# A pooling's means and differences on GpSimd, and eight modulation tiles used between its sums

## The chip, the cores and the metric

The kernel runs on one core of a Trainium2 chip. A core has TensorE (PE, matmuls), VectorE (DVE), ScalarE (ACT), GpSimd (POOL) and SyncE (SP), which run at the same time and wait for each other through semaphores. The metric is the time of one execution in microseconds (us). Data lie feature-major: 128 partitions by time steps, here T = 256.

## The reference, cut to what matters

Two network blocks follow each other on a 256 x 1024 input. The change lies in the second layer of the first block, a multi-scale pooling mixer, and in the modulation of the second block:

```python
z = h @ p["w_in"]                       # "ou" (u) and "og" (g): 16 tiles of 128 features each
u, g = jnp.split(z, [W_POOL], axis=-1)
# for each group of 512 features with its window w in (2, 4, 8, 16), in each row of 64 steps:
lo = jnp.clip(t - w // 2, 0, n); hi = jnp.clip(t + w // 2, 0, n)
d = (s[hi] - s[lo]) / cnt - u           # s is the running sum: window mean minus the value
y = einsum(d, p["w_grp"]) * p["scale"]  # "grp"
out = (y * jax.nn.silu(g)) @ p["w_out"] # "oa", "ob"
```

Second block: `mod = silu(c) @ w_mod + b_mod` and, for its first two parts, the same matrix again with `silu(c_ctx)`.

## The kernel before

**Weight tiles.** All weight matrices come as one stream of tiles of 128 x 1024 numbers (512 KB), in the order of the list ORDER, through a ring of six buffers `raw`. SyncE's queue loads tile n once tile n - 6 is finished on TensorE (semaphore tile_done). ScalarE rounds each tile to w_hi (L904, helper `highs`), VectorE takes w_lo = raw - w_hi (L1277, helper `lows`), and TensorE does each product in three parts, 24 matmuls for one tile (L547 to L549, helper `thirds`). A tile's product stands in one of four PSUM banks until ScalarE has emptied it (semaphore ps_free; `emptied` waits for that). On VectorE, `ahead(name, t)` makes all w_lo up to the tile four places behind (name, t).

**ou and og.** TensorE does ou 0 to 3 side by side, then ou 4 to 15 and og 0 to 15 one after the other, then the statistics of the context (two matmuls on sqx, which wait for GpSimd's sum), then grp 0 to 7 (L684), which needs the differences d_in (semaphore d_ready), and then oa and ob. ScalarE empties ou tile t into opad (L1117), a buffer with 8 zero columns on each side of each row of 64, and og tile t through SiLU into og (L1127).

**Pooling.** VectorE works in four groups of four ou tiles (L1656 to L1667). For group g it waits until tiles 4g to 4g + 3 are emptied, with the w_lo's of tiles 4g + 4 to 4g + 7 made on the way, and then `window(g)` adds opad to itself, shifted, in 1, 2, 3 or 4 steps (L1291 writing win0 and win1 in turn). A multiplication by 1/count gives the mean (L1291 writing d_in), and a subtraction of opad gives the difference (L1667).

**Modulation.** GpSimd's queue loads 80 modulation tiles (512 KB each, L436) into four slots modw, each load once the slot's last tile is used (modw_used). VectorE uses a tile by multiplying it with a row of silu(c) and summing along the free dimension. Tiles 32 to 47 (groups 8 to 11, here "modulation tiles 0 to 15") are used twice (L1648): into `dump` with the context's row and into modw with the other row. VectorE does so once in each of og 0 to 15, behind the w_lo of tile t + 4; for og 12 to 15 that w_lo doesn't exist, since the tiles four places behind are grp's. Behind this VectorE makes vr (L1610), multiplies grp's products with og (L1685) and takes y_lo (L1696).

**GpSimd's sums.** GpSimd also adds up squares for statistics (`add_up`, L458). Those of the second context (sqx) stand in its queue behind the loads of group 10. ScalarE makes these squares ahead of og 10 (L1125), when all four differences are done, since sqx lies over win0 and win1.

Of the kernel before, what the change touches and what calls it, by code (L numbers as in the profile page):

```python
# [22 lines left out]
ALU = mybir.AluOpType  # L23
ACT = mybir.ActivationFunctionType

P = 128
D = 1024
T = 256
KT = D // P
# [80 lines left out]
MOD_ORDER = list(range(MOD_TILES // MOD_SLOTS))  # L110
MOD_AT = {g: n for n, g in enumerate(MOD_ORDER)}


PARAMS = [
    ("norm_g", 16), ("mod_b", 48), ("ev_conv_w", 31 * 8), ("ev_conv_b", 8), ("ev_ln_g", 8), ("ev_ln_b", 8),
# [13 lines left out]
CON = {}  # L129
# [22 lines left out]
def build(nc, ins, out):  # L152
    with ExitStack() as ctx:
# [5 lines left out]
        def sem(name):  # L159
            return ctx.enter_context(nc.semaphore(name))  # L160
# [155 lines left out]
        h0_ready = sem("h0_ready")  # L316
        h_ready = sem("h_ready")
        u_ready = sem("u_ready")
        ga_ready = sem("ga_ready")
        shifts_in = [sem(f"shifts_in{j}") for j in range(2)]  # L320
        ya_raw, ya_rounded, ya_ready = sem("ya_raw"), sem("ya_rounded"), sem("ya_ready")
        yb_raw, yb_rounded, yb_ready = sem("yb_raw"), sem("yb_rounded"), sem("yb_ready")
# [60 lines left out]
        def emptied(eng, name, t):  # L383

            bank, before = PLACE[(name, t)]
            eng.wait_ge(ps_free[bank], before + 1)
# [42 lines left out]
        def _(pool):  # L429
            def loads(n):  # L430
                j, t = n % MOD_SLOTS, MOD_ORDER[n // MOD_SLOTS] * MOD_SLOTS + n % MOD_SLOTS
                if n >= MOD_SLOTS:
                    pool.wait_ge(modw_used[j], n // MOD_SLOTS)
                elif n == 0:
                    pool.wait_ge(mod0_in[KT - 1], 16)
                pool.dma_start(modw[j][:], ins["mod_w"][t]).then_inc(modw_in[j], 16)  # L436
# [13 lines left out]
            def add_up(bufs, signal, ready, n, step=1):  # L450

                before = [0] * len(bufs)
                for k in range(1, n):
                    for e, (dst, src) in enumerate(bufs):
# [6 lines left out]
                        else:  # L461
                            before[e] = M.do(a)

            copies_after = {3: (0,), 5: (1,), 7: (2, 3), 11: (4, 5), 15: (6,), 17: (7,)}
            for g in range(MOD_TILES // MOD_SLOTS):
                if g == 17:
                    pool.wait_ge(sg_act, 1)
                    add_up([(vn[:, 0, :], v2), (vsq[:, 0, :], vsq)], sg_act, 0, HEADS, 0)
                elif g == 19:
                    add_up([(sq4[:, 0, :], sq4)], sq_ready, 6 * KT, KT - 1)  # L470
                for n in range(g * MOD_SLOTS, (g + 1) * MOD_SLOTS):
                    loads(n)
                    for t in copies_after.get(n, ()):
                        shifted_copies(t)
                if g == 7:
                    add_up([(sq1[:, 0, :], sq1)], sq_ready, 2 * KT, KT - 1)
                elif g == 10:
                    add_up([(sqx[:, 0, :], sqx)], sq_ready, 3 * KT, KT - 1)
                elif g == 12:
                    add_up([(sq2[:, 0, :], sq2), (sqc[:, 0, :], sqc)], sq_ready, 4 * KT, KT - 1, 2)  # L480
# [786 lines left out]
        def _(v):  # L1267
# [13 lines left out]
            def ahead(name, t, by=4):  # L1281

                lows(*ORDER[min(TILE[(name, t)] + by, NTILES - 1)])
# [6 lines left out]
            def tt_(o, a, b, op):  # L1290
                return v.tensor_tensor(o, a, b, op)  # L1291
# [330 lines left out]

            def window(g):

                src = opad[:, 4 * g:4 * g + 4, :, :].rearrange("p a r c -> p (a r) c")
                w = WINDOWS[g]
                steps = [2]
                while steps[-1] < w:
                    steps.append(2 * steps[-1])
                for n, size in enumerate(steps):  # L1630
                    rest = sum(k // 4 for k in steps[n + 1:])
                    lo, hi_ = 8 - rest, 8 + GRID_W + rest
                    back, ahead = (1, 0) if size == 2 else (size // 4, size // 4)
                    S.do(tt_(win[n % 2][:, :, lo:hi_], src[:, :, lo - back:hi_ - back], src[:, :, lo + ahead:hi_ + ahead],
                             ALU.add))
                    S.sync()
                    src = win[n % 2]
                return src[:, :, 8:8 + GRID_W]

            def inner(g):  # L1640
                return opad[:, 4 * g:4 * g + 4, :, 8:8 + GRID_W].rearrange("p a r c -> p (a r) c")

            def second_mods(g, s, row, dst, t, last):

# [7 lines left out]
                else:  # L1652
                    S.do(a)

            v.wait_ge(crow_ready, 3)
            v.wait_ge(in_con2, 16)  # L1656
            for g in range(len(WINDOWS)):
                for t in range(4 * g, 4 * g + 4):
                    ahead("ou", t)
                    emptied(v, "ou", t)  # L1660
                mean = window(g)
                c0 = CON["inv_count"] + g * GRID_W
                inv = con[:, c0:c0 + GRID_W].rearrange("p (a c) -> p a c", a=1).to_broadcast([P, 16, GRID_W])
                dg = d_in[:, 4 * g:4 * g + 4, :].rearrange("p a (r c) -> p (a r) c", c=GRID_W)
                S.do(tt_(dg, mean, inv, ALU.mult))
                S.sync()
                v.tensor_tensor(dg, dg, inner(g), ALU.subtract).then_inc(d_ready, 1)  # L1667
            for g in range(8, 12):
                for s in range(MOD_SLOTS):
                    t = g * MOD_SLOTS + s  # L1670
                    ahead("og", t - 8 * MOD_SLOTS)
                    emptied(v, "og", t - 8 * MOD_SLOTS)
                    second_mods(g, s, 2, mod_c, t - 4 * KT, False)
                    second_mods(g, s, 0, mod, t, True)


            rstd(6, px[1][:, 0:T], D, EPS, vr[:, 0, :], vr[:, 3, :], 5)
# [422 lines left out]
```

## Time and profile before

| | |
|---|---|
| median of 3 runs | 955.75 us (955.3 to 956.18) |
| profiled execution, its own time | 957.27 us |
| its span | 955.5 us |
| granted TensorE clock, mean | 0.971 |
| TensorE busy | 889.3 us |
| VectorE busy | 710.1 us |
| GpSimd busy | 142.0 us |

The span is the time from the first to the last instruction that the profile shows. Rows of a timeline begin with the start in us from the span's start and the duration in us. An instruction may start before the one ahead of it has drained, so start-to-start intervals are the better measure of what one costs its engine. In brackets stands the time that the engine was idle before it, and what ended that.

### The profile page before, as it was taken

The numbers are of one execution on the slowest core, as the hardware profiler recorded it, in microseconds if no ns is written. First come the engines' busy times: TensorE is split into PE (matmuls) and PEld (weight loads), VectorE is DVE, ScalarE is ACT, GpSimd is POOL, SyncE is SP. The second block draws the span as 40 slices with busy tenths as digits, with TensorE's granted clock in tenths as the row PEclk, the third lists the DMA queues.
The fourth block names the chain that finished last, engine by engine and source line by source line (L and its number), as shares of the span: only waits on it lengthen the run. The fifth ranks groups of instructions, "written<-read, shape, count | busy, mean of one in ns | idle before, by whom it ended". The sixth has DMA issues, their size and how long they took to land.

```text
span 955.5 us, 16996 instructions
## 1 busy us (share of the span) xinstructions
PE 889.3 (93%) x6956; PEld 826.8 (87%) x6956; DVE 710.1 (74%) x1026; ACT 492.8 (52%) x701; POOL 142.0 (15%) x254
## 2 busy tenths in 40 slices
PE   5699999999897999899998999979999799999995
PEld 3388876689896999789998999979999699999995
DVE  3886567999886699988567975685986886666453
ACT  4634688896645544335553465463534454444441
POOL 0001865710021001410211100300001100000000
PEclk9699999999998999999999999999999899999998
DMA  9834977995576578775627744535465475566661
GB/s 371 347 111 119 297 236 233 284 326 196 143 272 230 198 222 270 252 275 174 182 89 265 284 133 144 193 107 178 155 184 169 130 236 185 179 182 188 200 198 48
DMA packets 56012, 195.51 MB, mean 205 GB/s; under 512 B 7936, under 2 KB 9088, under 8 KB 54528
## 3 DMA queue, kind: packets, MB, share of 16 engines
q1 hardware_dynamic: 40320, 147.83, 47.9%
q0 software_dynamic: 15616, 46.61, 14.3%
q8 instruction: 55, 0.90, 0.4%
q14 instruction: 21, 0.17, 0.1%
HBM read 188.70 MB, written 1.05 MB: 199 GB/s over the span
## 4 chain that ended last, share of the span: by engine, by line
PE 64%; DVE 18%; ACT 6%; DMA 5%; issue 4%; POOL 2%; SPq 1%; DVEq 0%; ACTq 0%; POOLq 0%
PE ps L547 19%; PE ps L549 18%; PE ps L548 18%; DVE w_lo L1277 6%; PE ps L684 3%; DMA m<-in_mod_w 2%; ACT w_hi L904 2%; DVE modw L1311 2%; DMA raw<-in_stream 2%; POOL shifts L445 2%; PE px L604 1%; DVE dump L1648 1%; DMA modw<-in_mod_w 1%; PE ps L615 1%; DVE li L1291 1%
## 5 line engine op out<-in xcount | busy, mean ns | idle before, releaser
L1277 DVE TENSOR_TENSOR w_lo<-raw,w_hi 128x1024 fp32r<-128x1024 f32 x232 | 281.2, 1225 | 132.6 <-ACT w_hi L904 132.2
L904 ACT ACTIVATE w_hi<-raw 128x1024 fp32r<-128x1024 f32 x232 | 243.6, 1056 | 131.4 <-DMA raw<-in_stream 131.2
L547 PE MATMUL ps<-h_hi,w_hi 128*128 128x256 f32 (+1 forms) x928 | 278.3, 300 | 27.6 <-DVE w_lo L1277 11.1
L548 PE MATMUL ps<-h_lo,w_hi 128*128 128x256 f32 (+1 forms) x928 | 273.0, 294 | 0.0
L549 PE MATMUL ps<-h_hi,w_lo 128*128 128x256 f32 (+1 forms) x928 | 272.7, 294 | 0.0
L547 PEld LDWEIGHTS ps<-h_hi,w_hi 128*128 128x128 f32 x928 | 181.0, 195 | 38.5 <-DVE w_lo L1277 17.5
L548 PEld LDWEIGHTS ps<-h_lo,w_hi 128*128 128x128 f32 x928 | 181.3, 195 | 4.0 <-issue 1.2
L549 PEld LDWEIGHTS ps<-h_hi,w_lo 128*128 128x128 f32 x928 | 181.1, 195 | 2.8
L547 PE MATMUL ps<-h2o_hi,w_hi 128*128 128x256 f32 x352 | 103.5, 294 | 8.5 <-DVE w_lo L1277 8.5
L548 PE MATMUL ps<-h2o_lo,w_hi 128*128 128x256 f32 x352 | 101.4, 288 | 0.0
L549 PE MATMUL ps<-h2o_hi,w_lo 128*128 128x256 f32 x352 | 101.3, 288 | 0.0
L436 POOL DMA_DIRECT2D modw<-in_mod_w x80 | 42.8, 536 | 325.3 <-DVE modw L1311 192.3
L1311 DVE SCALAR_TENSOR_TENSOR modw<-modw,c_row 128x1024 f32<-128x1024 f32 x64 | 76.6, 1230 | 7.2 <-DMA modw<-in_mod_w 7.1
L547 PEld LDWEIGHTS ps<-h2o_hi,w_hi 128*128 128x128 f32 x352 | 69.2, 197 | 9.7 <-DVE w_lo L1277 8.9
L445 POOL DMA_DIRECT2D shifts<-upad x128 | 62.7, 498 | 79.1 <-DVE upad L1431 73.2
L548 PEld LDWEIGHTS ps<-h2o_lo,w_hi 128*128 128x128 f32 x352 | 69.3, 197 | 0.3 <-issue 0.2
L549 PEld LDWEIGHTS ps<-h2o_hi,w_lo 128*128 128x128 f32 x352 | 69.3, 197 | 0.0
L458 POOL TENSOR_TENSOR sq<-sq 128x256 f32<-128x256 f32 x24 | 18.5, 770 | 329.0 <-ACT sq L1101 329.0
L548 PE MATMUL ps<-ff_lo,w_hi 128*128 128x256 f32 x176 | 49.8, 283 | 0.0
L547 PE MATMUL ps<-ff_hi,w_hi 128*128 128x256 f32 x176 | 49.8, 283 | 0.0
L549 PE MATMUL ps<-ff_hi,w_lo 128*128 128x256 f32 x176 | 49.8, 283 | 0.0
L1101 ACT ACTIVATE sq<-x 128x256 f32<-128x256 f32 x32 | 13.4, 418 | 67.7 <-DVE x L1599 67.7
(323 smaller groups left out, 1718.2 us busy)
## 6 DMA issues: line engine op xcount, KB each, us to landing
raw<-in_stream SPq DMA_DIRECT2D x252, 512.0 KB, 3.7
modw<-in_mod_w POOLq DMA_DIRECT2D x80, 512.0 KB, 6.1
m<-in_mod_w SPq DMA_DIRECT2D x8, 1024.0 KB, 16.2
shifts<-upad POOLq DMA_DIRECT2D x128, 35.5 KB, 3.9
c_row<-in_c_rows SPq DMA_DIRECT2D x3, 512.0 KB, 9.6
ctxT<-in_ctxT SPq DMA_DIRECT2D x1, 1024.0 KB, 5.0
x<-in_xT SPq DMA_DIRECT2D x1, 1024.0 KB, 7.1
ctx2T<-in_ctx2T SPq DMA_DIRECT2D x1, 1024.0 KB, 7.1
```

Of the source, the lines that this page charges most:

```text
L436: pool.dma_start(modw[j][:], ins["mod_w"][t]).then_inc(modw_in[j], 16)
L445: pool.dma_start(shifts[t % 2][32 * d:32 * d + 32, g, :], upad[32 * g:32 * g + 32, t % 3, d:d + RW]).then_inc(shifts_in[t % 2], 16)
L458: a = pool.tensor_tensor(dst, src[:, 0, :] if k == 1 else dst, src[:, k, :], ALU.add)
L547: pe.matmul(o, wh, hi, start=start, stop=False)
L548: pe.matmul(o, wh, lo, start=False, stop=False)
L549: return pe.matmul(o, wl, hi, start=False, stop=stop)
L604: mm = pe.matmul(px[b][:, :], w[:, 4 * e + b, :], xpad[:, head, :, SCONV_LEFT:SCONV_LEFT + T], start=True, stop=True)
L684: mm = pe.matmul(o[:, e * T:(e + 1) * T], w[:, 4 * e + k, :], d_in[:, 4 * (t // 2) + k, :], start=(k == 0), stop=(k == 3))
L904: act.activation(w_hi[split[0] % HI_RING][:], raw[n % RING][:], ACT.Copy).then_inc(w_hi_ready, 1)
L1101: act.activation(dst[:, t, :], x[:, t, :], ACT.Square).then_inc(sq_ready, 1)
L1277: v.tensor_tensor(w_lo[n % RING][:], raw[n % RING][:], w_hi[split[0] % HI_RING][:].bitcast(F32), ALU.subtract).then_inc(w_lo_ready, 1)
L1311: v.scalar_tensor_tensor(out=modw[s][:], in0=modw[s][:], scalar=1.0, in1=c_row[:, row, :], op0=ALU.mult, op1=ALU.mult, accum_out=mod[:, t: ...
```

## The change

GpSimd makes the mean and the difference of each group instead of VectorE, in the new function `mean_difference`. It waits for `window_ready`, which the last sum of each window signals. VectorE waits ahead of window g until g differences are done. The four calls stand in GpSimd's queue ahead of the loads of modulation tiles numbered 36, 38, 40 and 42. The sixteen modulation tiles used twice are spread anew: two behind each window (eight), one in each of og 0 to 7 (eight), none in og 8 to 15. The sum of sqx on GpSimd stands behind the loads of group 11 instead of group 10.

```diff
+MODS_AFTER = (0, 2, 4, 6, 8)
...
+            def mean_difference(g):
+
+                pool.wait_ge(window_ready, g + 1)
+                pool.wait_ge(in_con2, 16)
+                c0 = CON["inv_count"] + g * GRID_W
+                inv = con[:, c0:c0 + GRID_W].rearrange("p (a c) -> p a c", a=1).to_broadcast([P, 16, GRID_W])
+                dg = d_in[:, 4 * g:4 * g + 4, :].rearrange("p a (r c) -> p (a r) c", c=GRID_W)
+                n = M.do(pool.tensor_tensor(dg, win[g % 2][:, :, 8:8 + GRID_W], inv, ALU.mult))
+                M.sync(n)
+                centre = opad[:, 4 * g:4 * g + 4, :, 8:8 + GRID_W].rearrange("p a r c -> p (a r) c")
+                pool.tensor_tensor(dg, dg, centre, ALU.subtract).then_inc(d_ready, 1)
...
                 for n in range(g * MOD_SLOTS, (g + 1) * MOD_SLOTS):
+                    if n - 9 * MOD_SLOTS in MODS_AFTER[:len(WINDOWS)]:
+                        mean_difference(MODS_AFTER.index(n - 9 * MOD_SLOTS))
                     loads(n)
...
-                elif g == 10:
+                elif g == 11:
                     add_up([(sqx[:, 0, :], sqx)], sq_ready, 3 * KT, KT - 1)
...
             def window(g):
 
+                if g:
+                    v.wait_ge(d_ready, g)
...
-                    S.do(tt_(win[n % 2][:, :, lo:hi_], src[:, :, lo - back:hi_ - back], src[:, :, lo + ahead:hi_ + ahead],
-                             ALU.add))
-                    S.sync()
+                    a = tt_(win[n % 2][:, :, lo:hi_], src[:, :, lo - back:hi_ - back], src[:, :, lo + ahead:hi_ + ahead],
+                            ALU.add)
+                    if n == len(steps) - 1:
+                        a.then_inc(window_ready, 1)
+                    else:
+                        S.do(a)
+                        S.sync()
...
+            def both_rows(n):
+                t = 8 * MOD_SLOTS + n
+                second_mods(t // MOD_SLOTS, t % MOD_SLOTS, 2, mod_c, t - 4 * KT, False)
+                second_mods(t // MOD_SLOTS, t % MOD_SLOTS, 0, mod, t, True)
...
-                mean = window(g)
-                c0 = CON["inv_count"] + g * GRID_W
-                inv = con[:, c0:c0 + GRID_W].rearrange("p (a c) -> p a c", a=1).to_broadcast([P, 16, GRID_W])
-                dg = d_in[:, 4 * g:4 * g + 4, :].rearrange("p a (r c) -> p (a r) c", c=GRID_W)
-                S.do(tt_(dg, mean, inv, ALU.mult))
-                S.sync()
-                v.tensor_tensor(dg, dg, inner(g), ALU.subtract).then_inc(d_ready, 1)
-            for g in range(8, 12):
-                for s in range(MOD_SLOTS):
-                    t = g * MOD_SLOTS + s
-                    ahead("og", t - 8 * MOD_SLOTS)
-                    emptied(v, "og", t - 8 * MOD_SLOTS)
-                    second_mods(g, s, 2, mod_c, t - 4 * KT, False)
-                    second_mods(g, s, 0, mod, t, True)
+                window(g)
+                for s in range(MODS_AFTER[g], MODS_AFTER[g + 1]):
+                    both_rows(s)
+            for t in range(2 * KT):
+                ahead("og", t)
+                emptied(v, "og", t)
+                if t < 2 * KT - MODS_AFTER[-1]:
+                    both_rows(MODS_AFTER[-1] + t)
```

## Rows read from the trace of the kernel before

**Rows 1.** The page of the profile: each engine's busy us, share of the span, instructions

```profile
PE 889.3 (93%) x6956; PEld 826.8 (87%) x6956; DVE 710.1 (74%) x1026; ACT 492.8 (52%) x701; POOL 142.0 (15%) x254
```

**Rows 2.** Windows: busy us of PE, PEld, DVE, ACT, POOL; clock; DMA share, GB/s

```profile
318.00:360.00 42.00, 42.00 (x352) 42.00 (x351) 38.91 (x33) 22.32 (x32) 0.00 (x0) 1.00 0.73 242
360.00:407.00 47.00, 41.34 (x313) 39.31 (x312) 45.74 (x62) 17.30 (x31) 14.66 (x18) 0.96 0.80 263
...
418.00:440.00 22.00, 22.00 (x121) 19.91 (x120) 17.12 (x29) 9.75 (x14) 0.00 (x0) 1.00 0.59 195
```

**Rows 3.** Timeline of ACT: ou 7, og 0, og 5 and og 15 are emptied

```profile
328.28 0.39 ACT L1117 ACTIVATE opad<-ps 128x256 f32<-128x256 f32 x1 [0.53 <-PE ps L549]
...
354.20 0.38 ACT L1127 ACTIVATE og<-ps 128x256 f32<-128x256 f32 x1 [0.30 <-PE ps L549]
...
368.60 0.39 ACT L1127 ACTIVATE og<-ps 128x256 f32<-128x256 f32 x1 [0.29 <-PE ps L549]
...
407.12 0.38 ACT L1127 ACTIVATE og<-ps 128x256 f32<-128x256 f32 x1 [3.24 <-PE ps L549]
```

**Rows 4.** Timeline of DVE: start, duration, line, output<-inputs, from window 0 to the tail

```profile
322.90 1.22 DVE L1291 TENSOR_TENSOR win<-opad 128x1024 f32<-128x1024 f32 x1
324.15 1.22 DVE L1291 TENSOR_TENSOR d_in<-win,con 128x1024 f32<-128x1024 f32 x1
...
326.56 4.62 DVE L1277 TENSOR_TENSOR w_lo<-raw,w_hi 128x1024 fp32r<-128x1024 f32 x4
...
357.67 1.23 DVE L1291 TENSOR_TENSOR d_in<-win,con 128x1024 f32<-128x1024 f32 x1
...
360.07 1.22 DVE L1277 TENSOR_TENSOR w_lo<-raw,w_hi 128x1024 fp32r<-128x1024 f32 x1
...
385.40 1.22 DVE L1277 TENSOR_TENSOR w_lo<-raw,w_hi 128x1024 fp32r<-128x1024 f32 x1
386.54 1.22 DVE L1648 SCALAR_TENSOR_TENSOR dump<-modw,c_row 128x1024 f32<-128x1024 f32 x1
...
389.02 1.22 DVE L1277 TENSOR_TENSOR w_lo<-raw,w_hi 128x1024 fp32r<-128x1024 f32 x1
...
402.67 1.22 DVE L1277 TENSOR_TENSOR w_lo<-raw,w_hi 128x1024 fp32r<-128x1024 f32 x1
...
416.22 0.42 DVE L1610 TENSOR_SCALAR vr<-px 128x256 f32<-128x256 f32 x1
```

**Rows 5.** The chain of waits: start, us, what, number of instructions

```profile
407.95 27.63 PE ps L684 x128
```

**Rows 6.** Timeline of POOL: the six sqx additions, and two with DVE idle

```profile
389.94 9.25 POOL L458 TENSOR_TENSOR sqx<-sqx 128x256 f32<-128x256 f32 x6
...
458.28 0.73 POOL L458 TENSOR_TENSOR sq<-sq 128x256 f32<-128x256 f32 x1 [41.15 <-ACT sq L1101]
458.98 0.73 POOL L458 TENSOR_TENSOR sqc<-sqc 128x256 f32<-128x256 f32 x1
```

**Rows 7.** Timeline of DVE while GpSimd adds up sqx

```profile
390.15 1.76 DVE L1648 SCALAR_TENSOR_TENSOR dump<-modw,c_row 128x1024 f32<-128x1024 f32 x1
...
392.02 1.57 DVE L1648 SCALAR_TENSOR_TENSOR modw<-modw,c_row 128x1024 f32<-128x1024 f32 x1
...
393.52 1.73 DVE L1277 TENSOR_TENSOR w_lo<-raw,w_hi 128x1024 fp32r<-128x1024 f32 x1
...
400.19 1.21 DVE L1648 SCALAR_TENSOR_TENSOR dump<-modw,c_row 128x1024 f32<-128x1024 f32 x1
```

**Rows 8.** DMA issues of 318 to 420: modulation tiles, KB, median us to landing

```profile
modw<-in_mod_w POOLq DMA_DIRECT2D x16, 512.0 KB, 5.9
```

**Rows 9.** Timeline of PE: the first matmul of og 12 and of og 13

```profile
390.29 0.39 PE L547 MATMUL ps<-h_hi,w_hi 128*128 128x256 f32 x1 [0.48 <-DVE w_lo L1277]
...
395.31 0.42 PE L547 MATMUL ps<-h_hi,w_hi 128*128 128x256 f32 x1 [1.88 <-DVE w_lo L1277]
```

**Rows 10.** Windows of PE alone: og 13, busy us, granted clock

```profile
395.30:399.80 4.50, 4.49 (x24) 0.62 0.22 90
```

More of the change, by code:

```diff
@@ L318, in build @@
         u_ready = sem("u_ready")
-        ga_ready = sem("ga_ready")
+        ga_ready, window_ready = sem("ga_ready"), sem("window_ready")
         shifts_in = [sem(f"shifts_in{j}") for j in range(2)]
@@ L1633, in window @@
                     back, ahead = (1, 0) if size == 2 else (size // 4, size // 4)
-                    S.do(tt_(win[n % 2][:, :, lo:hi_], src[:, :, lo - back:hi_ - back], src[:, :, lo + ahead:hi_ + ahead],
-                             ALU.add))
-                    S.sync()
+                    a = tt_(win[n % 2][:, :, lo:hi_], src[:, :, lo - back:hi_ - back], src[:, :, lo + ahead:hi_ + ahead],
[5 more added lines that the diff above has]
+                        S.sync()
                     src = win[n % 2]
-                return src[:, :, 8:8 + GRID_W]
-            def inner(g):
-                return opad[:, 4 * g:4 * g + 4, :, 8:8 + GRID_W].rearrange("p a r c -> p (a r) c")
             def second_mods(g, s, row, dst, t, last):
@@ L1653, in second_mods @@
                     S.do(a)
+            def both_rows(n):
+                t = 8 * MOD_SLOTS + n
+                second_mods(t // MOD_SLOTS, t % MOD_SLOTS, 2, mod_c, t - 4 * KT, False)
+                second_mods(t // MOD_SLOTS, t % MOD_SLOTS, 0, mod, t, True)
             v.wait_ge(crow_ready, 3)
-            v.wait_ge(in_con2, 16)
             for g in range(len(WINDOWS)):
```

## Prediction

> **What bounds the kernel now.** I read the page first [rows 1]: TensorE is busy for 93% of the span and VectorE for 74%. These are averages over stages, so they don't say what a cut in VectorE's work is worth here. The windows of the stages that the change touches say more [rows 2]. In ou (318 to 360) TensorE never stops, and VectorE is busy for 38.91 of 42 us. In og (360 to 407) TensorE is busy for 41.34 of 47 and VectorE for 45.74. So VectorE has little room in ou, and in og it is the bound.
>
> ScalarE empties every product tile, which gives TensorE's pace [rows 3]. The reader is to see three spans. From ou 7 (328.28) to og 0 (354.20) lie 9 tiles in 25.92 us, 2.88 each. From og 0 to og 5 (368.60) it is 2.88 again. From og 5 to og 15 (407.12) 10 tiles take 38.52, which is 9.7 more than 10 x 2.88. Those 9.7 us are all that a faster VectorE could win in og.
>
> VectorE's timeline [rows 4] shows why. One og tile takes it 385.40 to 389.02, 3.62 us: a w_lo (1.14 from start to start) and one tile of modulation, used twice (2.48). It is slower than 2.88, so each w_lo comes late, after the lead of four tiles is used up. But w_lo of og 15 starts at 402.67, og 15 ends at 407.1, and VectorE goes on to 416.22 with modulation tiles 12 to 15. That tail (4 x 2.48 = 9.9) costs nothing now: TensorE does the grp product meanwhile, in 27.63 us without a break, from 407.95 [rows 5], and it stays busy for all of 418 to 440 [rows 2].
>
> **What leaves VectorE.** Each group's two operations on d_in go: 324.15 to 326.56 and 357.67 to 360.07 [rows 4], 2.4 us; four groups are 9.6 us. Each window's last sum no longer waits for itself. A synced operation starts 1.25 after the one before, an unsynced one 1.14, so this is 4 x 0.11 = 0.4.
>
> **What is moved.** Before, eight modulation tiles stand ahead of w_lo of og 12 (those used in og 0 to 7), four more ahead of w_lo of og 15, and four behind. After, all sixteen stand ahead of w_lo of og 12: two behind each of the four window sums, one in each of og 0 to 7. So ahead of w_lo of og 12 come 8 x 2.48 = 19.8 us more, which already outweighs the 10.0 taken away. From og 12 on VectorE has only w_lo's, and TensorE sets the pace.
>
> Where does VectorE's lateness start to count? In ou the first two tiles of modulation come between window 0 and w_lo of ou 8, which now starts at 326.56 [rows 4]. TensorE has finished ou 7 by 328.28 [rows 3]. So w_lo of ou 8 has 0.6 us to spare at its end, and 4.97 us are put ahead of it. From there on I expect VectorE's queue, never idle, to be the chain up to w_lo of og 12. Its own waits for emptied ou tiles don't bind, because TensorE runs four tiles in 11.5 us and VectorE needs longer for its share of them.
>
> **What GpSimd's work costs VectorE.** This is the largest term, and the trace has one place for it: GpSimd's six additions for sqx. They take 9.25 us in all, against 0.70 us from start to start when VectorE is idle (458.28, 458.98) [rows 6]. In that time VectorE's operations grow too [rows 7]: from 390.15 to 400.19 it does two rounds of dump, modw and w_lo in 10.04 us, where two rounds at 3.62 are 7.24. It loses 2.8 us to six GpSimd operations, 0.47 each. The two engines take turns.
>
> The new operations are 128x1024, four times as wide, eight of them. No row shows GpSimd at that width. Below, VectorE loses 0.47 each if only the handover costs (3.7 in all), or nothing. If the loss grows with the width it is 1.87 each (15.0). If each further element costs a whole idle element (0.70/256), it is 0.47 + 768 x 0.00273 = 2.57 (20.5). A strided GpSimd operation might take twice as long: 4 each (32). I take 2.0 each, 16.0 us, near the proportional value: 0.23 of the 0.70 is already free of loss, so it is the rest that should scale.
>
> The Trainium skill's page "SBUF — State Buffer" (Who interferes with whom) says that a VectorE instruction with two SBUF inputs and a GpSimd instruction that reads SBUF exclude each other for the whole instruction. The trace's turns agree with it. Its "GPSIMD Engine Reference" (Elementwise — side-by-side cycle accounting) gives 4497 ns for a GpSimd add of 2048 elements; an estimate by that page is 2.25 us for 1024 elements, and by it the loss would be 18 us and the time about 981.5.
>
> The sqx additions stay and move to behind group 11's loads. ScalarE makes their squares once og 9 is out, about three og tiles before the end of VectorE's chain, so about five of the six fall on it: 5 x 0.47 = 2.3. Before, they fell behind w_lo of og 12.
>
> **The new waits.** Window g waits for the difference g - 1. Behind it on VectorE stand the window, two modulation tiles and the next w_lo, and TensorE waits for that. Between window g - 1 and window g VectorE has 4 x 1.14 + 4.97 = 9.5 us of its own plus what GpSimd's two operations take from it. GpSimd needs those same two spans plus at most two VectorE operations' turns (2.3). So this wait should be short or absent. Modulation tile 10 needs a load queued on GpSimd behind the last difference. That is 2 x (1.14 + 2.1) = 6.5, plus an issue, plus 5.9 to landing [rows 8], some 13 us after window 3. VectorE comes to it after 4.97 + 4.0 + 2 x 3.62 + 1.14 = 17.3. No wait, with 4 us to spare. ScalarE's wait for all four differences comes at og 10 and TensorE's at grp, both later still. The loads on SP's queue are paced by finished tiles, which come later; nothing waits for them.
>
> **The sum,** against the profiled execution.
> - Start of the work behind w_lo of og 12, before: 390.15. After: - 9.6 - 0.4 + 19.8 + 16.0 + 2.3 = + 28.1, at 418.3.
> - From there to og 15's end, before: 407.1 - 390.15 = 16.9. After: four tiles on TensorE, 3 x 2.88 + 3.15 (the last tile now: w_lo ends 403.9, out at 407.1) = 11.8. That gives - 5.1.
> - The clock: w_lo of og 13 comes 1.88 us late and the matmuls behind it take 0.42 us instead of 0.28 [rows 9]. For that tile the granted clock averages 0.62, where 0.5 is 1.2 GHz and 1 is 2.4 GHz, and its 24 matmuls fill 4.49 us, 1.6 more than 2.88 [rows 10]. The bigger gaps (about 6 us at ou 8, ou 12, og 0 and og 4) are absorbed in VectorE's chain; one near og 12, while the sqx additions slow VectorE, may not be. I take half of it, 0.8.
> - Total + 23.8. grp then starts 23.8 later, with the same work behind it.
>
> The profiled span is 955.5 and the median is 955.75; I add to the median: **979.5 us**. Without any loss to GpSimd's new work the sum would be + 7.8, so the placement alone makes it slower.
>
> **The rivals.**
> 1. *GpSimd costs little (0 to 0.47 each).* Then 963.5 to 967.3. For it: only the 256-wide form was seen. Against it: VectorE's lost time there is two thirds of GpSimd's idle-engine time, more than a handover should take. Chance 0.14.
> 2. *GpSimd is slow with the strided rows of win and opad,* 4 us lost each: + 39.8, so 995. Nothing in the trace speaks for or against it; all the additions seen have plain rows. Chance 0.11.
> 3. *Not slower: the tail was on the path.* If VectorE's end at 416.22 set when y and so the oa product comes, then taking 9.6 us off VectorE and moving the tail forward would be a pure gain, up to 946. It decides only if grp's end hangs on VectorE and if GpSimd costs nothing. Against it stand the 128 grp matmuls without a gap [rows 5]. Chance 0.05.
> 4. *My forecast,* own range 974 to 986 (1.4 to 2.7 us per operation). Chance 0.70.
>
> The range that leaves out less than 2 in 10 reaches toward rivals 1 and 2: 966 to 990. Less than 0.2% (1.9 us) is about what a measurement here can't tell from no change. Faster 0.04, same 0.02, slower 0.94.
>
> **What the changed profile would show.** GpSimd has eight 128x1024 operations, each over 2 us and some over 3 where VectorE's turn comes first. VectorE's dump and modw operations behind each window take about 3 us instead of 1.22, four times two of them. ScalarE empties ou 8 about 6 us later than now, og 15 about 24 us later, and the last four og tiles come 2.88 apart. TensorE waits for w_lo in ou, where it now never does. No long wait of VectorE on GpSimd's semaphore. grp takes 27.6 us again. I am wrong if VectorE's operations stay near 1.22 beside the new ones (rival 1), if they exceed 5 us (rival 2), or if the w_lo of ou 8 is not what TensorE waits for.

## The result, and the profile after

The changed kernel takes 980.85 us (977.8 to 981.69, 4 runs), the kernel before 955.96 (955.3 to 957.32, 4 runs): ratio 1.0255 with a 95% interval of 1.0236 to 1.0273, so 22.6 to 26.1 us slower. The forecast was + 23.8 and 979.5. The profiled execution is the shortest of the four (977.8, span 975.7).

The page, beside [rows 1]: GpSimd is busy for 27 us more, and VectorE for 7 us more, though 10 us of its work were taken away.

```profile
PE 894.0 (92%) x6956; PEld 831.9 (85%) x6956; DVE 717.4 (74%) x1018; ACT 492.3 (50%) x701; POOL 169.1 (17%) x262
```

The windows, beside [rows 2], with the same columns. TensorE, which never stopped in ou, is now busy for 32.88 of 42 us there, and for 38.49 of the next 50, while VectorE is busy for 40.02 and 48.85. In grp and behind (430 to 460) TensorE is full again.

```profile
318.00:360.00 42.00, 32.88 (x248) 32.47 (x247) 40.02 (x35) 17.42 (x26) 18.55 (x9) 0.88 0.63 207
360.00:410.00 50.00, 38.49 (x281) 37.48 (x280) 48.85 (x56) 16.62 (x27) 14.44 (x12) 0.90 0.70 230
...
430.00:460.00 30.00, 30.00 (x152) 26.75 (x151) 17.66 (x29) 9.99 (x16) 0.00 (x0) 1.00 0.52 159
```

VectorE's timeline beside [rows 4] and [rows 7]:

```profile
321.72 1.22 DVE L1308 TENSOR_TENSOR win<-opad 128x1024 f32<-128x1024 f32 x1
322.85 1.22 DVE L1667 SCALAR_TENSOR_TENSOR dump<-modw,c_row 128x1024 f32<-128x1024 f32 x1
...
324.19 3.23 DVE L1667 SCALAR_TENSOR_TENSOR modw<-modw,c_row 128x1024 f32<-128x1024 f32 x1
...
327.35 3.36 DVE L1667 SCALAR_TENSOR_TENSOR dump<-modw,c_row 128x1024 f32<-128x1024 f32 x1
...
330.82 1.23 DVE L1667 SCALAR_TENSOR_TENSOR modw<-modw,c_row 128x1024 f32<-128x1024 f32 x1
...
331.98 4.63 DVE L1294 TENSOR_TENSOR w_lo<-raw,w_hi 128x1024 fp32r<-128x1024 f32 x4
...
384.79 1.22 DVE L1294 TENSOR_TENSOR w_lo<-raw,w_hi 128x1024 fp32r<-128x1024 f32 x1
...
410.13 1.75 DVE L1294 TENSOR_TENSOR w_lo<-raw,w_hi 128x1024 fp32r<-128x1024 f32 x1
...
415.17 6.22 DVE L1294 TENSOR_TENSOR w_lo<-raw,w_hi 128x1024 fp32r<-128x1024 f32 x4
```

The first dump behind window 0 takes its usual 1.22 us, since it started ahead of GpSimd's first operation. The next modw starts at 324.19 and the dump after it at 327.35, 3.16 us later instead of 1.15. That dump's modw starts at 330.82, 3.47 later instead of 1.33. The losses are 2.01 and 2.14; in the other three groups they are 2.01 to 2.02 and 2.14 to 2.20, 16.7 us in all. w_lo of ou 8, which started at 326.56 before, starts at 331.98. From 384.79 on GpSimd is idle and an og tile takes 3.62 again, and from 410.13 it adds up sqx.

GpSimd's timeline beside [rows 6]: each 128x1024 operation takes 3.2 to 3.3 us. The first starts at 323.02, while VectorE's dump of 322.85 runs on to about 324.0, so I read about 1.1 us of each as waiting for VectorE's running operation and the rest as its own.

```profile
323.02 3.31 POOL L474 TENSOR_TENSOR d_in<-win,con 128x1024 f32<-128x1024 f32 x1 [26.82 <-DVE win L1308]
326.41 3.22 POOL L477 TENSOR_TENSOR d_in<-d_in,opad 128x1024 f32<-128x1024 f32 x1
...
409.61 9.57 POOL L461 TENSOR_TENSOR sqx<-sqx 128x256 f32<-128x256 f32 x6 [9.43 <-ACT sqx L1142]
```

TensorE's timeline beside [rows 9]: the number in brackets is how long it was idle for w_lo of ou 8, ou 12, og 0, og 4 and og 12.

```profile
333.25 0.58 PE L564 MATMUL ps<-h_hi,w_hi 128*128 128x256 f32 x1 [6.24 <-DVE w_lo L1294]
...
349.40 0.39 PE L564 MATMUL ps<-h_hi,w_hi 128*128 128x256 f32 x1 [2.88 <-DVE w_lo L1294]
...
366.91 0.39 PE L564 MATMUL ps<-h_hi,w_hi 128*128 128x256 f32 x1 [4.25 <-DVE w_lo L1294]
...
386.06 0.58 PE L564 MATMUL ps<-h_hi,w_hi 128*128 128x256 f32 x1 [5.88 <-DVE w_lo L1294]
...
416.96 0.38 PE L564 MATMUL ps<-h_hi,w_hi 128*128 128x256 f32 x1 [1.89 <-DVE w_lo L1294]
```

ScalarE's timeline beside [rows 3]: ou 8, og 11, og 12 and og 15 are emptied. ou 8 comes at 337.92. From og 12 to og 15 the tiles are 2.88 apart.

```profile
337.92 0.38 ACT L1134 ACTIVATE opad<-ps 128x256 f32<-128x256 f32 x1 [8.24 <-PE ps L566]
...
415.11 0.38 ACT L1144 ACTIVATE og<-ps 128x256 f32<-128x256 f32 x1 [1.58 <-PE ps L566]
420.14 0.39 ACT L1144 ACTIVATE og<-ps 128x256 f32<-128x256 f32 x1 [4.65 <-PE ps L566]
...
428.78 0.38 ACT L1144 ACTIVATE og<-ps 128x256 f32<-128x256 f32 x1 [2.50 <-PE ps L566]
```

Window 0 starts at slightly different times in different executions (322.90 before, 321.72 after), so I compare by the time from there to og 15: 84.2 us before and 107.1 after, + 22.8. The rest of the span, from og 15 to the end, is 548.4 before and 546.9 after.

### The profile page after: what moved, and what is told of

Read it like the earlier page. It is cut to its first block, busy times and chain, and to the rows that moved or that the text cites. A ratio compares the mean times of both kernels' runs of the same rounds, so it can differ in the third digit from the quotient of the medians.

```text
span 975.7 us, 17008 instructions
## 1 busy us (share of the span) xinstructions
PE 894.0 (92%) x6956; PEld 831.9 (85%) x6956; DVE 717.4 (74%) x1018; ACT 492.3 (50%) x701; POOL 169.1 (17%) x262
## 4 chain that ended last, share of the span: by engine, by line
PE 60%; DVE 21%; ACT 6%; issue 5%; DMA 5%; POOL 2%; SPq 1%; DVEq 0%; ACTq 0%; POOLq 0%
PE ps L564 17%; PE ps L566 17%; PE ps L565 17%; DVE w_lo L1294 7%; DVE dump L1667 3%; PE ps L701 3%; DMA m<-in_mod_w 2%; ACT w_hi L921 2%; DVE modw L1328 2%; POOL shifts L448 2%; DMA raw<-in_stream 1%; PE px L621 1%; DMA modw<-in_mod_w 1%; PE ps L632 1%; DVE win L1308 1%
## 5 line engine op out<-in xcount | busy, mean ns | idle before, releaser
L564 PEld LDWEIGHTS ps<-h_hi,w_hi 128*128 128x128 f32 x928 | 183.8, 198 | 55.6 <-DVE w_lo L1294 34.5
L565 PEld LDWEIGHTS ps<-h_lo,w_hi 128*128 128x128 f32 x928 | 183.9, 198 | 3.9 <-issue 1.2
L566 PEld LDWEIGHTS ps<-h_hi,w_lo 128*128 128x128 f32 x928 | 183.8, 198 | 2.7
L1118 ACT ACTIVATE sq<-x 128x256 f32<-128x256 f32 x32 | 13.4, 418 | 67.2 <-DVE x L1616 67.2
## 6 DMA issues: line engine op xcount, KB each, us to landing
m<-in_mod_w SPq DMA_DIRECT2D x8, 1024.0 KB, 16.1
```

The source lines that it names most:

```text
L564: pe.matmul(o, wh, hi, start=start, stop=False)
L565: pe.matmul(o, wh, lo, start=False, stop=False)
L566: return pe.matmul(o, wl, hi, start=False, stop=stop)
L1118: act.activation(dst[:, t, :], x[:, t, :], ACT.Square).then_inc(sq_ready, 1)
```

## The experiments

The question was whether the two terms of the sum (placement, GpSimd's turns) are each what I said, what exactly takes VectorE's time, and where time could be won instead. The table has all runs. "Before" is the median of the kernel before as it was run beside each of them, on the same chip; it lies between 953.89 and 955.96. "Window 0 to og 15" is read from each trace as above, as a difference to the 84.2 us of before.

| run | median us | before | ratio to before, 95% interval | window 0 to og 15 |
|---|---|---|---|---|
| the changed kernel | 980.85 | 955.96 | 1.0255 [1.0236, 1.0273] | + 22.8 |
| e8, the changed kernel again | 981.37 | 955.46 | 1.0279 [1.0250, 1.0309] | + 24.7 |
| e1, placement only | 973.9 | 953.89 | 1.0219 [1.0194, 1.0244] | + 18.0 |
| e2, GpSimd only | 964.93 | 953.89 | 1.0108 [1.0077, 1.0140] | + 6.8 |
| e3, widths (one execution) | 971.68 | 953.89 | | + 15.1 |
| e4, GpSimd only writes | 963.38 | 953.89 | 1.0101 [1.0082, 1.0121] | + 7.9 |
| e5, five tiles late | 974.03 | 955.46 | 1.0192 [1.0158, 1.0226] | + 17.4 |
| e6, spread | 954.62 | 955.46 | 0.9994 [0.9975, 1.0013] | - 9.3 |
| e7, spread, GpSimd | 961.11 | 955.46 | 1.0062 [1.0040, 1.0085] | - 2.0 |
| e9, statistics behind grp | 952.53 | 955.07 | 0.9986 [0.9969, 1.0004] | - 9.7 |
| e10, context modulation late | 953.47 | 955.65 | 0.9973 [0.9955, 0.9991] | - 9.5 |
| e11, two more w_lo's | 954.0 | 955.33 | 0.9989 [0.9976, 1.0002] | - 9.8 |

**e1: the placement alone.** To the kernel before, in VectorE's part (and the sqx sum behind group 11):

```diff
                 v.tensor_tensor(dg, dg, inner(g), ALU.subtract).then_inc(d_ready, 1)
-            for g in range(8, 12):
-                for s in range(MOD_SLOTS):
-                    t = g * MOD_SLOTS + s
-                    ahead("og", t - 8 * MOD_SLOTS)
-                    emptied(v, "og", t - 8 * MOD_SLOTS)
-                    second_mods(g, s, 2, mod_c, t - 4 * KT, False)
-                    second_mods(g, s, 0, mod, t, True)
+                for s in range(2 * g, 2 * g + 2):
+                    both_rows(s)
+            for t in range(2 * KT):
+                ahead("og", t)
+                emptied(v, "og", t)
+                if t < 8:
+                    both_rows(8 + t)
```

> The sixteen modulation tiles are placed as in the changed kernel (two behind each window, one in each of og 0 to 7, sqx summed behind group 11), but VectorE makes the means and differences as before. My theory (placement and GpSimd's turns add up): the median is that of before plus 19.8 + 2.3 - 5.1 = 17.0, about 973 us (971 to 975). Rival A (the loss is nearly all contention, the placement is free): under 960. Rival B (the changed kernel's loss comes from placement alone, GpSimd's work being a wash): about 981.

VectorE's first window and ScalarE's og 15, whose distance is the number that I compare:

```profile
320.74 1.22 DVE L1291 TENSOR_TENSOR win<-opad 128x1024 f32<-128x1024 f32 x1
```

```profile
422.99 0.38 ACT L1127 ACTIVATE og<-ps 128x256 f32<-128x256 f32 x1 [2.50 <-PE ps L549]
```

+ 18.0 by the trace, where the sum had 17.0. In this trace the clock falls beside og 12, so the tile takes longer (it is emptied 6.5 us after og 11, against 5.0 in the changed kernel's first trace), and that makes 1.5 of it. By the medians it is + 20.0 against the kernel before on the same chip; the 2 us between the two numbers have no explanation in the traces, since none of the kernel before was taken on that chip. Both rivals are out either way.

**e2: GpSimd alone.** To the changed kernel:

```diff
-                    if n - 9 * MOD_SLOTS in MODS_AFTER[:len(WINDOWS)]:
-                        mean_difference(MODS_AFTER.index(n - 9 * MOD_SLOTS))
+                    if n == 9 * MOD_SLOTS:
+                        for w_ in range(len(WINDOWS)):
+                            mean_difference(w_)
...
-                elif g == 11:
+                elif g == 10:
...
                 window(g)
-                for s in range(MODS_AFTER[g], MODS_AFTER[g + 1]):
-                    both_rows(s)
...
-                if t < 2 * KT - MODS_AFTER[-1]:
-                    both_rows(MODS_AFTER[-1] + t)
+                both_rows(t)
```

> GpSimd makes the means and differences, with all four in its queue ahead of the load numbered 36; the sixteen modulation tiles stay in og 0 to 15 as before. My theory: VectorE loses 8 x 2.07 = 16.6 us (the price that the changed kernel's trace shows) and is spared 10.0, so about + 6.6, 962.5 us (960.5 to 964.5), and the VectorE operations beside GpSimd's are now w_lo subtractions of about 3.2 us. Rival A (contention is everything): + 20 or more. Rival B (GpSimd's work is free): - 10, about 946.

+ 6.8 by the trace, 6.6 expected. In part that is luck: VectorE's rows show 17.5 us lost (4.4 for each four w_lo's, so 2.2 for each GpSimd operation, not 2.07) and 10.1 spared, and 0.6 of short waits of VectorE for w_hi, which the kernel before has in ou, are gone. VectorE's timeline shows that w_lo is blocked in the same way as the modulation: window 0, then four w_lo's in 9.0 us instead of 4.6, then window 1.

```profile
320.66 1.22 DVE L1309 TENSOR_TENSOR win<-opad 128x1024 f32<-128x1024 f32 x1
321.80 9.05 DVE L1295 TENSOR_TENSOR w_lo<-raw,w_hi 128x1024 fp32r<-128x1024 f32 x4
330.77 1.25 DVE L1309 TENSOR_TENSOR win<-opad 128x1056 f32<-128x1056 f32 x1
```

The median moved by more than the trace, 11.0 us. The four executions are 960.5 (the profiled one), 964.3, 965.5 and 967.2 us, with mean granted clocks of 0.972, 0.970, 0.965 and 0.965. A fall of the mean from 0.972 to 0.965 is 1.4% of the span spent at the lower level, 13.4 us in which TensorE does half the work: 6.7 us lost, and 967.2 is 6.7 above 960.5. That is an estimate, and it fits the others less well: 965.5 has the same clock of 0.965 and is only 5.0 above, and for 964.3 the same count gives 1.9 of 3.8. So the clock accounts for the excess only roughly. No trace of the longer executions shows which tiles.

The two effects add up in the traces: 18.0 + 6.8 = 24.8, and the changed kernel's second trace (e8) has 24.7. By the medians they don't: 20.0 + 11.0 = 31.0, where the changed kernel has 24.9 and in e8 25.9. So that the two terms add up rests on one trace of each kernel, and why the medians of e1 and e2 stand some 2 and 4 us above their traces stays open.

**e3 and e4: what takes VectorE's time.** e3 cuts GpSimd's operations to fewer rows in groups 1 to 3 (most means and differences are left out):

```diff
+                k = (16, 8, 4, 1)[g]
+                if k < 16:
+                    M.do(pool.memset(dg[:, k:], 0.0))
-                n = M.do(pool.tensor_tensor(dg, win[g % 2][:, :, 8:8 + GRID_W], inv, ALU.mult))
+                n = M.do(pool.tensor_tensor(dg[:, 0:k], win[g % 2][:, 0:k, 8:8 + GRID_W], inv[:, 0:k], ALU.mult))
...
-                pool.tensor_tensor(dg, dg, centre, ALU.subtract).then_inc(d_ready, 1)
+                pool.tensor_tensor(dg[:, 0:k], dg[:, 0:k], centre[:, 0:k], ALU.subtract).then_inc(d_ready, 1)
```

> The changed kernel with GpSimd's two operations cut to fewer rows of 64: full width (1024) in group 0, 512 in group 1, 256 in group 2, 64 in group 3; the rest of d_in is set to zero by a memset, so most means and differences are left out. One look. If the loss grows with the elements, VectorE's stretched operations grow by about 2.05, 1.0, 0.5 and 0.1 us in the four groups. If each operation also has a fixed part of the turn, by 2.05, 1.15, 0.7 and 0.35. If only the handover cost, all four would be alike, which the full width already speaks against. Time between 966 and 972 us.

VectorE's timeline: the modw and the dump beside a GpSimd operation 512, 256 and 64 wide.

```profile
341.07 2.12 DVE L1670 SCALAR_TENSOR_TENSOR modw<-modw,c_row 128x1024 f32<-128x1024 f32 x1
...
343.12 2.31 DVE L1670 SCALAR_TENSOR_TENSOR dump<-modw,c_row 128x1024 f32<-128x1024 f32 x1
...
356.38 1.57 DVE L1670 SCALAR_TENSOR_TENSOR modw<-modw,c_row 128x1024 f32<-128x1024 f32 x1
...
357.89 1.75 DVE L1670 SCALAR_TENSOR_TENSOR dump<-modw,c_row 128x1024 f32<-128x1024 f32 x1
...
372.26 1.22 DVE L1670 SCALAR_TENSOR_TENSOR modw<-modw,c_row 128x1024 f32<-128x1024 f32 x1
...
373.41 1.34 DVE L1670 SCALAR_TENSOR_TENSOR dump<-modw,c_row 128x1024 f32<-128x1024 f32 x1
```

From start to start they lose 0.90 and 1.09 at 512, 0.36 and 0.53 at 256, and 0.00 and 0.12 at 64, against 2.01 and 2.14 at 1024. From 256 to 1024 that is 2.1 ns for each further element, and carried back to no elements it leaves nothing fixed. In sum VectorE loses 7.1 us instead of 16.7; 24.7 - 9.6 gives 15.1 for window 0 to og 15, and the trace has 15.1. (Both traces have the slower tile at og 12, emptied 6.5 us after og 11.)

e4 lets GpSimd write the same 128x1024 region without reading anything (all means and differences are left out):

```diff
-                n = M.do(pool.tensor_tensor(dg, win[g % 2][:, :, 8:8 + GRID_W], inv, ALU.mult))
+                n = M.do(pool.memset(dg, 0.0))
...
-                pool.tensor_tensor(dg, dg, centre, ALU.subtract).then_inc(d_ready, 1)
+                pool.memset(dg, 1.0).then_inc(d_ready, 1)
```

> The changed kernel with GpSimd's two operations for each group replaced by two memsets of the same 128x1024 region of d_in, so that means and differences are left out and GpSimd reads nothing from SBUF. If what blocks VectorE is GpSimd's reading (VectorE's second input and GpSimd's input through one interface), every VectorE operation behind a window stays near 1.22 us and the time falls by 8 x 2.07 = 16.6 to about 964 us. Rival: any GpSimd operation blocks VectorE, writes too: VectorE operations still grow by most of a memset's duration and the time stays above 970.

GpSimd's timeline, then VectorE's at the same time:

```profile
323.07 0.95 POOL L474 MEMSET d_in<- 128x1024 f32 x1 [26.73 <-DVE win L1308]
324.08 0.96 POOL L477 MEMSET d_in<- 128x1024 f32 x1
```

```profile
324.27 1.23 DVE L1667 SCALAR_TENSOR_TENSOR modw<-modw,c_row 128x1024 f32<-128x1024 f32 x1
...
325.42 1.22 DVE L1667 SCALAR_TENSOR_TENSOR dump<-modw,c_row 128x1024 f32<-128x1024 f32 x1
```

Two memsets run beside three VectorE operations, none of which grows, and the time falls to 963.38. By the traces it falls by 24.7 - 7.9 = 16.8, the whole price of GpSimd's turns, and the + 7.9 that is left is the + 7.8 that the sum had without any loss to GpSimd (there with half a slow tile, here with a whole one). So GpSimd's being busy, and its writing, do not hold VectorE's two-input operations up. What the memset lacks is the reading. The run changes the kind of operation along with it, so by this run alone the reading is named by elimination. The Trainium skill's page "SBUF — State Buffer" (Who interferes with whom) says just this: against a GpSimd instruction that only writes, such a VectorE instruction does not contend. This run agrees, with 1.22 to 1.23 us for each.

**e5: is placement a matter of the sum or of the order?** To the changed kernel (and the sqx sum behind group 10):

```diff
-                if t < 2 * KT - MODS_AFTER[-1]:
-                    both_rows(MODS_AFTER[-1] + t)
+                if t < 3:
+                    both_rows(8 + t)
+                elif t >= 11:
+                    both_rows(t)
```

> The changed kernel, but the last five of the sixteen modulation tiles are used in og 11 to 15, behind w_lo of og 15, as the kernel before has them (three are used in og 0 to 2, none in og 3 to 10; sqx summed behind group 10 again). My theory: TensorE's idle time in ou and at og 0 and og 4 is lost for good, and from about og 7 on TensorE sets the pace; the chain up to w_lo of og 7 ends at about 397, nine tiles later og 15 is out at about 424, where the changed kernel has 428.8. So - 5 against the changed kernel, about 976 us (973 to 978). Rival (only the sum of VectorE's work ahead of the last w_lo counts): five tiles moved behind it give 5 x 2.48 = 12.4, 968.5.

```profile
321.52 1.22 DVE L1308 TENSOR_TENSOR win<-opad 128x1024 f32<-128x1024 f32 x1
```

```profile
423.10 0.38 ACT L1144 ACTIVATE og<-ps 128x256 f32<-128x256 f32 x1 [2.50 <-PE ps L566]
```

974.0 against 981.4 for e8 on the same chip: 7.3 less by the medians, 7.3 by the traces as well (17.4 against 24.7). 1.5 of that is the tile at the lower clock that e8 has and e5 has not, which leaves 5.8, near the 5 expected and far from 12.4. TensorE's waits at ou 8, ou 12, og 0 and og 4 were the same (6.0, 2.8, 4.3 and 5.9 us). Once a w_lo is late, taking work away further on gives back only what TensorE still waits for there.

**e8: the changed kernel's second trace, and the clock.**

> The changed kernel once more, for its trace beside the others on the same chip. The sum left open whether a late w_lo near og 12 halves TensorE's clock for a tile. In the first trace it did not (span 975.7), and the three other executions were 3 us longer with lower mean granted clocks. If the clock is the cause, this trace has either a span near 976 and a clock near 0.965, or a span near 979 and a clock near 0.961 with one or more tiles of 24 matmuls that take 4.5 us instead of 2.9 behind a late w_lo. Rival: longer spans at the same clock, with the time in some other stage.

Span 979.3, clock 0.962. TensorE waits for w_lo of og 12 for 1.89 us, as in the first trace (416.96 above):

```profile
418.39 0.39 PE L564 MATMUL ps<-h_hi,w_hi 128*128 128x256 f32 x1 [1.89 <-DVE w_lo L1294]
```

The windows of og 12 in TensorE's rows, first the changed kernel's first trace, then this one (us, busy us and number of matmuls, granted clock, DMA share, GB/s):

```profile
416.90:420.10 3.20, 3.14 (x26) 1.00 0.28 104
```

```profile
418.30:423.00 4.70, 4.61 (x26) 0.64 0.79 268
```

The same wait, and once the clock stays at 1.00, once it averages 0.64 and the tile takes 1.5 us longer. That accounts for most of the 1.9 us between the two traces' times to og 15. The rest of the 3.6 us between the spans lies ahead of window 0 (1.1) and behind og 15 (0.7).

**e6 and e7: using the room.** An og tile leaves VectorE 2.88 - 1.14 = 1.74 us, 0.7 of a modulation tile. e6 is the kernel before with the sixteen tiles spread by that rule, and a second dump buffer in the place of opad for grp:

```diff
+PAIRS_OG = (0, 1, 3, 4, 6, 7, 9, 10, 12, 13, 14)
+PAIRS_GRP = (0, 1, 2, 3, 4)
...
+        dump2 = at("dump2", W + 28, [D])
...
-            for g in range(8, 12):
-                for s in range(MOD_SLOTS):
-                    t = g * MOD_SLOTS + s
-                    ahead("og", t - 8 * MOD_SLOTS)
-                    emptied(v, "og", t - 8 * MOD_SLOTS)
-                    second_mods(g, s, 2, mod_c, t - 4 * KT, False)
-                    second_mods(g, s, 0, mod, t, True)
+            for t in range(2 * KT):
+                ahead("og", t)
+                emptied(v, "og", t)
+                if t in PAIRS_OG:
+                    both_rows()
...
                                     ALU.subtract).then_inc(y_ready, 2)
+                if t in PAIRS_GRP:
+                    in_grp[0] = True
+                    v.wait_ge(d_ready, len(WINDOWS))
+                    both_rows()
```

> Built on the kernel before, pooling wholly on VectorE: of the sixteen modulation tiles eight are used in og 0, 1, 3, 4, 6, 7, 9 and 10 (0.7 for each og tile, which is what 2.88 - 1.14 leaves room for), three in og 12 to 14 behind w_lo of og 15, and five in the grp loop, where VectorE was idle 4.9 of 22 us. My theory: TensorE then runs og at 2.88 a tile nearly throughout and grp stays at 27.6 us, so up to the 9.7 us lost in og come back: 946 to 950 on the scale of before 955.75, ratio 0.990 to 0.995. Rival (VectorE's whole work up to the end of y is the bound, wherever it stands): TensorE waits in grp or at oa for w_lo and y instead, no more than 2 us faster.

```profile
320.38 1.22 DVE L1294 TENSOR_TENSOR win<-opad 128x1024 f32<-128x1024 f32 x1
```

```profile
395.33 0.38 ACT L1130 ACTIVATE og<-ps 128x256 f32<-128x256 f32 x1 [2.49 <-PE ps L552]
```

og 15 comes 9.3 us earlier (74.95 behind window 0, against 84.22), and the time stays the same: 0.9994. The first half of my theory held and the second fell. TensorE's timeline shows two waits that the kernel before doesn't have:

```profile
400.31 1.03 PE L514 MATMUL px<-sqx,ones_p 128*128 128x256 f32 x2 [5.02 <-POOL sqx L461]
...
449.71 0.39 PE L550 MATMUL ps<-y_hi,w_hi 128*128 128x256 f32 x1 [1.69 <-DVE w_lo L1280]
```

5.02 us go to GpSimd's sum of sqx, which the statistics ahead of grp need, and 1.69 to a w_lo in oa. The long wait costs more than itself: from og 15 to the first matmul of oa it is 28.1 us in the kernel before and 35.1 here, some 2 us more than the wait explains, and in the 10 us behind the wait the granted clock averages 0.83. VectorE starts the context's modulation 120.6 us behind window 0 in the kernel before and 121.2 here. The gain went into waits further on, and into the slower clock behind one of them.

> The same spread as in the run before it, with means and differences on GpSimd as in the changed kernel. My theory: GpSimd's operations still take 8 x 2.07 from VectorE in ou and give back 10.0, so w_lo's come 6.6 us later by og 0 and about half of this is caught up by the end of og: 3 to 7 us slower than the run before it. Rival (with VectorE no longer short of time in og, the offload is free or a gain): equal or faster.

e7 puts `mean_difference` into e6 in the way of e2. It is 6.5 us slower than e6 by the medians, 7.2 by the traces. The time is inside what I expected, but not by the way that I gave: nothing is caught up by the end of og. With room in og, GpSimd's help still costs VectorE more than it spares.

**e9, e10 and e11: following the gain.** e9 to e6 (on ScalarE the root and w_hi of ob 2 and 3 move along):

```diff
             for t in range(2 * KT):
                 thirds("og", t, *h1)
-            two_chunks(px[1], sqx, 2, 4 * KT)
...
                 mm.then_inc(tile_done, 1)
+            two_chunks(px[1], sqx, 2, 4 * KT)
             for t0_ in range(0, KT, 4):
...
-            rstd(6, px[1][:, 0:T], D, EPS, vr[:, 0, :], vr[:, 3, :], 5)
             for t in range(KT + 1):
...
             lows("oa", 3)
             lows("ob", 1)
+            rstd(6, px[1][:, 0:T], D, EPS, vr[:, 0, :], vr[:, 3, :], 5)
+            lows("ob", 3)
```

> The spread kernel (modulation tiles in og 0, 1, 3, 4, 6, 7, 9, 10, 12 to 14 and grp 0 to 4, pooling on VectorE), and in addition the two matmuls of the context's statistics, with VectorE's vr and ScalarE's root, stand behind grp instead of ahead of it, and w_hi and w_lo of ob 2 and ob 3 are made ahead of the context's modulation. The spread kernel's trace wins 9.3 us by og 15 and gives back 4.9 waiting for GpSimd's sum of sqx ahead of grp and the rest at oa and ob, where VectorE is late. My theory: with grp free of the statistics it runs from og 15 on, and oa's and ob's w_lo's come in time; oa 4 starts about 9 us earlier against window 0 than in the kernel before. So 946 to 950 us on the scale of before 955.75, ratio 0.990 to 0.995. Rival (VectorE's whole work up to the context's modulation is the bound, wherever it stands): ratio within 0.998 to 1.001 again, with TensorE waiting for w_lo or a bank at oa 4.

grp now starts right behind og 15, but TensorE waits for a bank at oa 4, which add_to_x on VectorE frees:

```profile
450.30 0.36 PE L550 MATMUL ps<-y_hi,w_hi 128*128 128x256 f32 x1 [4.30 <-DVE x L1601]
```

e10 to e9 (ScalarE's `sqrt_of` and `shifted` move along, with `highs`):

```diff
-            rstd(6, px[1][:, 0:T], D, EPS, vr[:, 0, :], vr[:, 3, :], 5)
             lows("ob", 3)
...
-            modulate(KT, ctx2T, vr[:, 3, :], sc2[1], sh2[1], t2, h2c_hi, h2c_lo)
             S.sync()
             for t in range(KT):
+                if t == 4:
+                    lows("oa", 7)
+                    rstd(6, px[1][:, 0:T], D, EPS, vr[:, 0, :], vr[:, 3, :], 5)
+                    modulate(KT, ctx2T, vr[:, 3, :], sc2[1], sh2[1], t2, h2c_hi, h2c_lo)
                 add_to_x("ob", t, gate1)
```

> The run before (spread, statistics behind grp) reached oa 4 at 446.0 and then waited 4.3 us for its bank, which add_to_x of ob 0 frees, because VectorE did the context's root and modulation (434 to 448.5) first. Here these stand behind add_to_x of ob 3, beside oa 4 to ob 7. My theory: the 4.3 us come back, and most of the 9 us won in og reach the end: 946 to 950 us on the scale of before 955.75, ratio 0.990 to 0.995. Rival (VectorE's sum of work through ob is the bound): TensorE stalls later in oa or ob instead and the ratio stays at 0.998.

```profile
466.31 0.58 PE L550 MATMUL ps<-y_hi,w_hi 128*128 128x256 f32 x1 [4.78 <-DVE w_lo L1281]
```

e11 to e10 (the same on ScalarE with `highs`):

```diff
                     rstd(6, px[1][:, 0:T], D, EPS, vr[:, 0, :], vr[:, 3, :], 5)
+                    lows("ob", 5)
                     modulate(KT, ctx2T, vr[:, 3, :], sc2[1], sh2[1], t2, h2c_hi, h2c_lo)
```

> The run before, whose trace has TensorE waiting 4.8 us at 466.3 for w_lo of ob 4, since VectorE's root and modulation of the context (453.4 to 464.6) take longer than the lead of four tiles. Here w_hi and w_lo of ob 4 and ob 5 are made between the root and the modulation. My theory: those 4.8 us come back, 948 to 951 us on the scale of before 955.75, ratio 0.992 to 0.996. Rival (the gain is lost again at the next place where VectorE is late): ratio 0.997 as in the run before, with another wait of 3 us or more further on.

```profile
466.37 0.39 PE L550 MATMUL ps<-y_hi,w_hi 128*128 128x256 f32 x1 [1.56 <-DVE w_lo L1282]
...
478.05 0.70 PE L514 MATMUL px<-sq,ones_p 128*128 128x256 f32 x2 [2.80 <-POOL sqc L461]
...
480.48 1.22 PE L516 MATMUL px<-sq,ones_p 128*128 128x256 f32 x2 [1.72 <-ACT sqc L1143]
```

Each step removed the wait that it was made for, and another took its place: w_lo of ob 4 (4.78), then a shorter wait for w_lo (1.56) and waits for GpSimd's and ScalarE's squares of x (2.80, 1.72). Behind the long wait of each trace the granted clock is lower for a stretch, as in e6: 0.79 from 450 to 458 in e9, 0.82 from 466 to 475 in e10, and 0.77 from 475 to 490 in e11. From window 0 to the start of the next stage's h (the first h2o_hi) it is 167.0 us in the kernel before, 167.5 in e6, 165.2 in e9, 163.8 in e10 and 165.1 in e11. So of 9.3 to 9.8 us won in og nothing reaches the end of the layer in e6, and about 2 to 3 us do in e9 to e11. e10 has the best ratio, 0.9973 with an interval of 0.9955 to 0.9991. It beats the changed kernel clearly and the kernel before by about a quarter of a per cent, at the edge of what can be told: it is the best of four such ratios, and e9 and e11, which differ little from it, can't be told from before. The rival was nearer than my theory in all four expectations, though not in everything: e11's asked for another wait of 3 us or more, and the longest is 2.80.

## Why the prediction was right

- **What leaves VectorE, what is moved.** Right in sum: e1 gives + 18.0 with a tile at the lower clock (1.5), where the sum had 17.0 without one. One count in the text was off: ahead of w_lo of og 15 the kernel before has three further modulation tiles, not four, and five behind it, not four. The tail that cost nothing was therefore 5 x 2.48 = 12.4 us (403.81 to 416.22), not 9.9. The sum took this stretch from rows as 16.9 us, so no number moved.
- **The start of the chain.** w_lo of ou 8 is what TensorE waits for first, 6.24 us, and VectorE is never idle from window 0 to w_lo of og 12. From window 0 to the start of the work behind that w_lo I had 418.3 - 322.9 = 95.4 us; the matmuls behind it start 95.2 after window 0.
- **GpSimd's price.** 2.01 to 2.20 us for each operation, 2.09 on the average, against 2.0 taken; 16.7 in all against 16.0. e3 shows that it grows with the elements, as I took it to. The estimate by the Trainium skill's page "GPSIMD Engine Reference" (Elementwise — side-by-side cycle accounting), 18 us, was a little high. The reasoning by "the rest scales" was right in its size, but the trace of before could not show it, and rivals 1 and 2 were rightly priced as open.
- **sqx.** Five additions on the chain were forecast. VectorE's rows from 410.13 to 415.17 lose 1.4 us and the w_lo behind them 0.5: 1.9 instead of 2.3.
- **The clock.** 0.8 was half of 1.6. In the first trace nothing is lost there, in e8 and e1 the tile behind a late w_lo takes 1.5 us longer. The cost comes in whole tiles, and half was too little: seven traces (before, the changed kernel twice, e1 to e4) have one such wait of 1.88 or 1.89 us in og, and in six of them the tile behind it ends 6.5 us after the one ahead; only the changed kernel's first trace has 5.0. The mean granted clocks of its four executions (0.965 in the shortest, 0.961 to 0.963 in the others) suggest that most of them pay as well. So + 22.8 in the first trace is the sum without its clock term (23.0), and with a whole tile the sum would be 24.5, where the medians have + 24.9. That + 23.8 lies between is a matter of taking the middle.
- **What cancels.** GpSimd's price was 0.7 too low and the sqx term 0.4 too high. The mechanism is right term by term, but the sum is closer than its terms by that much luck.
- **No new wait.** VectorE has no row that waits for GpSimd's differences, and modulation tile 10 (393.16) follows without a gap. grp and the stage behind it are as full as before.
- **The gaps.** I gave about 6 us for each of ou 8, ou 12, og 0 and og 4. They are 6.24, 2.88, 4.25 and 5.88. From the end of each of these waits to the end of the next it is 16.1, 17.5 and 19.2 us, set by VectorE's chain, and TensorE's four tiles fill 13.3 of each instead of the 11.5 that I took: the granted clock is down to 0.88 to 0.90 on the average of these stretches. A slower TensorE there only shortens its wait, since w_lo comes when VectorE's chain has it.

What stays open is what no trace covers: e2's executions differ by 6.7 us, of which the clock explains a part, and the medians of e1 and e2 add up to 31.0 us where their traces add up to 24.8.

## What to carry to other kernels

Before handing VectorE's work to GpSimd, look at what both read. If VectorE's operations beside it take two inputs from SBUF and GpSimd's read too, they take turns, and here each element (fp32, two inputs) costs VectorE 2.1 to 2.2 ns to save it about 1.2. That is a loss wherever VectorE is short of time. No run here has a VectorE operation with one input beside such work.

When one engine prepares tiles for another, what counts is the work ahead of each tile, not the sum over the stage: work moved from behind the last tile to ahead of the first is paid in full, and what is removed later gives back only what is still being waited for (5.8 of 12.4 us in e5). And a gain inside a stage is worth what the next stage lets through: follow it to the end before counting it.

## What the runs showed of the hardware that I had not expected

The same wait of 1.89 us on TensorE, at the same place of the same program, was followed by the full clock in one execution and by a tile at a mean of 0.64 in another, where the matmuls up to the eighth follow each other in about 0.12 us and those from the ninth on in 0.21. Six of seven traces with such a wait have the slow tile. Waits of 6 us at ou 8 and og 4 and of 4.3 at og 0 are absorbed wherever the chain runs through VectorE, so in ou and og of the changed kernel the clock costs only at the last late tile.

GpSimd's memset of 128x1024 took 0.95 us beside VectorE's two-input operations, and its two-input operations of the same size 3.2 to 3.3, a third of which I read as waiting for its turn.
